# Second block of a two-block transformer: rounds cut into finer steps, queues reordered, projection tiles a round ahead, output halves in separate banks

## The reference, cut to what matters

```
a = rmsnorm(h, g_pre_mix);  u = a @ w_in
c_val, c_gate, q, k, v = split(u)                 # 512 columns each; 8 heads of 64
glu = c_val * sigmoid(c_gate)
y   = causal depthwise conv(glu, 31 taps) + conv_b          # 512 channels
conv_out = silu(layernorm(y))
z = q @ k.T / 8;  strictly causal mask
attn = exp(log_sigmoid(z) + reverse_cumsum_between(log_sigmoid(-z)))   # stick-breaking
attn_out = rmsnorm_per_head(attn @ v)
h = h + rmsnorm(concat(conv_out, attn_out) @ w_out)
h = h + rmsnorm((silu(f @ w_gate) * (f @ w_up)) @ w_down),  f = rmsnorm(h)
```

## Time and profile before

| what | us |
|---|---|
| three runs, median (lowest to highest) | 2006.15 (2003.53 to 2006.83) |
| the profiled execution | 2003.01 |
| its span in the trace | 2001.2 |
| PE busy in the span | 1849.5 (92%) |
| DVE busy | 957.3 (48%) |
| ACT busy | 769.7 (38%) |
| POOL busy | 159.7 (8%) |

### The profile page before, as it was taken

How to read it: one execution, slowest core, us unless ns; L and a number is a source line. 1 busy time by engine, 2 the same in 40 slices (tenths; PEclk the granted TensorE clock), 3 DMA queues, 4 the chain that set the end, 5 groups by cost and what they waited for, 6 DMA issues and landing times.

```text
span 2001.2 us, 21728 instructions
## 1 busy us (share of the span) xinstructions
PE 1849.5 (92%) x8477; PEld 1509.3 (75%) x8477; DVE 957.3 (48%) x1702; ACT 769.7 (38%) x1517; POOL 159.7 (8%) x204
## 2 busy tenths in 40 slices
...
GB/s 221 74 64 64 95 85 98 103 95 96 95 102 82 53 53 43 22 43 85 96 99 94 101 95 96 73 95 22 32 11 1 94 65 96 100 100 95 95 95 42
DMA packets 195749, 158.37 MB, mean 79 GB/s; under 512 B 5248, under 2 KB 161152, under 8 KB 195648
## 3 DMA queue, kind: packets, MB, share of 16 engines
...
## 4 chain that ended last, share of the span: by engine, by line
PE 80%; DVE 13%; ACT 5%; issue 2%; DMA 0%; SPq 0%; ACTq 0%; DVEq 0%
PE ps L727 26%; PE ps L728 25%; PE ps L729 25%; DVE sb L2174 3%; DVE sb L1779 2%; PE ps L777 1%; DVE sb L2293 1%; DVE sb L2225 1%; ACT sb L1626 0%; PE ps L1156 0%; DVE sb L1777 0%; DVE sb L1939 0%; PE ps L1044 0%; DVE sb L1805 0%; PE ps L1020 0%
## 5 line engine op out<-in xcount | busy, mean ns | idle before, releaser
L727 PE MATMUL ps<-sb,sb 128*128 128x512 f32 (+3 forms) x2547 | 1002.2, 396 | 45.3 <-DVE sb L2212 13.5
L728 PE MATMUL ps<-sb,sb 128*128 128x512 f32 (+3 forms) x2547 | 977.6, 386 | 0.0
L729 PE MATMUL ps<-sb,sb 128*128 128x512 f32 (+3 forms) x2547 | 977.1, 385 | 0.0
L727 PEld LDWEIGHTS ps<-sb,sb 128*128 128x128 f32 (+1 forms) x2547 | 486.2, 192 | 158.2 <-DVE sb L2212 14.4
L729 PEld LDWEIGHTS ps<-sb,sb 128*128 128x128 f32 (+1 forms) x2547 | 486.3, 192 | 94.2
L728 PEld LDWEIGHTS ps<-sb,sb 128*128 128x128 f32 (+1 forms) x2547 | 487.6, 193 | 87.8
L1779 DVE TENSOR_TENSOR sb<-sb,sb 128x512 fp32r<-128x512 f32 x532 | 356.2, 711 | 359.7 <-ACT sb L1292 358.6
L1292 ACT ACTIVATE sb<-sb 128x512 fp32r<-128x512 f32 x532 | 304.7, 622 | 453.6 <-PE ps L729 453.6
L1978 DVE TENSOR_TENSOR sb<-sb,sb 128x512 fp32r<-128x512 f32 x64 | 68.1, 1063 | 176.9 <-ACT sb L1434 176.9
L1444 ACT ACTIVATE sb<-ps 128x512 f32<-128x512 f32 x64 | 38.4, 599 | 208.3 <-PE ps L729 208.3
L633 POOL TENSOR_TENSOR sb<-sb 128x512 f32<-128x512 f32 x64 | 66.9, 1045 | 607.9 <-ACT sb L1444 607.9
...
## 6 DMA issues: line engine op xcount, KB each, us to landing
...
```

The costliest lines, as they stand in the source:

```text
L727: mm(ps, lh, rh, start=start, stop=False, **k)
L728: mm(ps, lh, rl, start=False, stop=False, **k)
L729: return mm(ps, ll, rh, start=False, stop=stop, **k)
```

## The change

The list `PLAN_C` is written anew, in these parts:

- **Tiles.** `v2` (the convolution's value tile), `q1` and `k1` move from the rounds into the fill phase, which now has twelve tiles. The four that are left (`q2 k2 q3 k3`) stand at the end of rounds 0 to 3, and the three convolution groups and `ln_sub` at the end of rounds 4 to 7 (`BEHIND`). Eviction (`ev`), splitting (`lo`) and weights (`w`) are steps of their own; a tile is evicted at the start of the next round.
- **Steps.** The ACT and DVE parts of `sp`, `bt` and `va` are cut: `sp` (DVE), `ex` (ACT exp of the head before), `sl` (split of the soft-plus), `ah` and `at` (split of the attention), `kp` (keep). PE runs `lg(u)`, `bt(u-1)`, `va(u-2)` and then the tile.
- **Diagonals.** ACT no longer builds any; POOL builds whole parts of a group at once with `tensor_tensor` on broadcast operands, high and low.
- **Pair sums** are made in bank 6 instead of bank 7, and `va` waits for their reading.
- **End.** The output product's slab order is pairs first (`[4,5],[6,7],[0,1],[2,3]`); its first slab is run early inside the list (`out_first`, step `o`); silu and its splits go row by row. Its second half accumulates in banks 4 to 7.

```diff
-    IN_FIRST = ["g0", "v0", "g3", "v3", "g1", "v1", "g2", "q0", "k0"]
-    IN_LATER = ["q1", "v2", "k1", "q2", "k2", "q3", "k3"]
+    IN_FIRST = ["g0", "v0", "g3", "v3", "g1", "v1", "g2", "v2", "q0", "k0", "q1", "k1"]
+    IN_LATER = ["q2", "k2", "q3", "k3"]
...
-        CH["out", n] = chunk([(W["w_out_2"][0], 512 * n, 512)], [[4, 5], [0, 1], [2, 3], [6, 7]])
+        CH["out", n] = chunk([(W["w_out_2"][0], 512 * n, 512)], [[4, 5], [6, 7], [0, 1], [2, 3]])
...
+        PLAN_C += [("tile", x), ("w", SL["in", x] + 3), ("ev", x), ("lo", x), ("taps", 5 if n >= 2 else 0)]
     for j in range(4):
+        PLAN_C += [("v2", j), ("w", CH["v2"].first + min(j, 2) + 3), ("taps", 4)]
     PLAN_C += [("v2_out",)]
+    BEHIND = [("tile", x) for x in IN_LATER] + [("cv", g) for g in range(3)] + [("ln_sub",)]
+    for u in range(8):
+        b = BEHIND[u - 1] if u else ("", "")
+        if b[0] == "tile":
+            PLAN_C += [("ev", b[1])]
+        elif b[0] == "cv":
+            PLAN_C += [("co", b[1])]
+        PLAN_C += [("lg", u), ("taps", 2)]
+        if u >= 4:
+            PLAN_C += [("pt" if u % 2 else "ps", u // 2 - 2)]
+        PLAN_C += [("taps", 2)]
+        if u >= 1:
+            PLAN_C += [("bt", u - 1)]
         if u >= 2:
             PLAN_C += [("va", u - 2)]
+        PLAN_C += [("sp", u)]
+        if u >= 1:
+            PLAN_C += [("ex", u - 1)]
+        if b[0] == "tile":
+            PLAN_C += [("lo", b[1])]
         if u >= 4 and u % 2 == 0:
+            PLAN_C += [("pr", u // 2 - 2)]
+        PLAN_C += [("sl", u)]
+        if u >= 1:
+            PLAN_C += [("ah", u - 1), ("at", u - 1)]
+        if u >= 2:
+            PLAN_C += [("kp", u - 2)]
+        PLAN_C += [BEHIND[u]]
+        if u < 5:
+            PLAN_C += [("w", CH["v2"].last + min(u, 3) + 4)]
+        if u >= 4 and u % 2:
+            PLAN_C += [("pl", u // 2 - 2)]
+        PLAN_C += [("taps", 2 if u < 6 else 100)]
+    PLAN_C += [("bt", 7), ("ps", 2), ("va", 6), ("ex", 7), ("pr", 2), ("o", (0, 1, 2)), ("ah", 7), ("at", 7), ("kp", 6),
+               ("ln_var",), ("pt", 2), ("ln_rs",), ("va", 7), ("kp", 7), ("pl", 2), ("ps", 3), ("pr", 3), ("ln_mul",),
+               ("o", (3,)), ("pt", 3), ("silu", 0), ("pl", 3)]
+    for j in range(1, 4):
+        PLAN_C += [("silu", j), ("ll", j - 1)]
+    PLAN_C += [("ll", 3)]
...
-                    e.tensor_scalar(DL[:, k % 16, :], IDENT, CWL[:, k:k + 1], None, ALU.mult).then_inc(S("dl"), 1)
+                    q.wait_ge(S("w_used"), SL["in", "k3"] + 1)
...
+                    if part[0] >= 16:
+                        q.wait_ge(S("cv_used"), 1 + (part[-1] >= 26))
...
+                    for dst, w in ((DH, CWH[:, at].bitcast(F32)), (DL, CWL[:, at])):
+                        TTT(dst[:, k0:k0 + n, :], eye, w.unsqueeze(2).broadcast_to([128, n, 128]), ALU.mult).then_inc(
...
-                act(ATh[:, :], TT[:, :], ACT.Copy).then_inc(S("at_hi"), 1)
-            elif kind == "va":
+            elif kind == "ah":
+                u = a[0]
                 q.wait_ge(S("sb_exp"), 3 * u + 3)
                 q.wait_ge(S("values"), u)
                 act(ATh[:, :], TT[:, :], ACT.Copy).then_inc(S("at_hi"), 1)
+            elif kind == "kp":
...
-        tile_n(CH["out", 0], M2h, M2l, mixed_ready, 0, lambda t: None)
-        tile_n(CH["out", 1], M2h, M2l, mixed_ready, 0, lambda t: q.wait_ge(S("f_ev"), t + 1))
+        tile_n(CH["out", 0], M2h, M2l, mixed_ready, 0, lambda t: None, done=1)
+        q.wait_ge(S("keep"), 8)
+        tile_n(CH["out", 1], M2h, M2l, mixed_ready, 4, lambda t: None)
```

More of the change, by code:

```diff
@@ L407, in build @@
     assert PAIR_NORMS == [("pair", s[1]) if s[0] == "pr" else ("ln",) for s in PLAN_C if s[0] in ("pr", "ln_rs")]
-    IN_7 = [s for i, s in enumerate(PLAN_C) if s[0] in ("cv", "ps", "pt", "ln_sub", "ln_var", "ln_mul")
-            or s[0] == "tile" and s[1] in IN_LATER]
+    IN_7 = [s for s in PLAN_C if s[0] in ("cv", "pt", "ln_sub", "ln_var", "ln_mul") or s[0] == "tile" and s[1] in IN_LATER]
     class Mem:
@@ L587, in out_of_7 @@
             return S("cv_ev"), step[1] + 1
-        if kind == "ps":
-            return S("rs_v"), USE["pair", step[1]] + 1
         if kind == "pt":
@@ L1231, in block_step @@
                 m.then_inc(S("ln_ps"), 1)
-        for step in PLAN_C:
-            block_step(*step)
         def mixed_ready(k):
```

149 lines of the change are left out of this document (69 added, 80 removed).

## The result

| | median, us | lowest to highest | runs |
|---|---|---|---|
| before | 2004.84 | 1997.91 to 2006.83 | 4 |
| changed | 1947.26 | 1946.32 to 1949.60 | 4 |

The ratio is 0.9721, with a 95% interval of 0.9695 to 0.9746: 2.8% faster. The forecast was 1943 us, with a range of 1931 to 1968. The profiled execution took 1949.6 us, its span is 1947.8 us, and PE is busy for 1833.5 us of it (94%).

What follows compares the result with a forecast made beforehand. The prediction took the order of work between fill phase and output product, where PE waits, as the bound. Its walk gave 62.9 us less: 2003.0 to 1940, plus 3.1 for the median, 1943 us; likeliest 1931 to 1952, with rivals to 1968.

Steps and rivals of the forecast that it cites:

- the likeliest case: Whole kernel: the forecast itself holds, 1931 to 1952 us, chance 0.62.
- the walk: Sum of stages from fill phase to output product's end, which moves from 1601.4 to 1538.5: 62.9 us less.
- Fill phase: Three more tiles before the first logits, paced by DVE: a cost of 19.3 us, first logits at 1356.6.
- the rival of a clock lost there: Fill phase: PE's short waits bring 1.2 GHz, some eight tiles slow down, 31 us more, 1974 us; chance 0.05.
- Round 0: First bank 7 tile still waits, until 1362.9, then takes 7.4 us; round 1 begins at 1370.3.
- Rounds 1 to 3: PE waits for nothing: 11.75 us for round 1, 13.75 each for rounds 2 and 3.
- 5 to 6 us to spare: Round 2 check: ACT's and DVE's splits `sl` and `at` are ready 5 to 6 us before PE needs them.
- Rounds 4 to 6: A convolution group and a `ps` or `pt` replace the tile: 16.5 us each, `pt` no longer stalls.
- 2.5 to 3.6 ns an element: Price taken for POOL's wide diagonal builds: first group 6.5 to 9.3 us against 9.4 available.
- hidden, or about 1 us late: POOL's diagonal builds before the convolution groups: they cost PE nothing or about 1 us.
- Tail: Logits of round 7 to output product's end: 79.4 us, last `pt` waiting for DVE until 36.6.
- Second half in its own banks: Output product's second half in separate banks: brings nothing, since PE had no gap between the halves.

Runs made afterwards that it cites:

- e11: Changed kernel with the weights and five taps around DVE's reading of the pair sums moved to the end of round 4; 1942.65 us, ratio 0.9690.
- e4: Kernel before with only the tiles moved: three into the fill phase, four to the end of rounds 0 to 3; 1982.26 us, ratio 0.9912.
- e7: Changed kernel with eviction and split of a late tile at the end of its own round instead of the next; 1953.93 us, ratio 0.9756.
- e3: Changed kernel with the old order of steps within a round (keep, soft-plus and its split first, then exp); 1960.12 us, ratio 0.9778.
- e10: Changed kernel with the pair's transposes (pt) of pairs 0 and 1 in the round of their sums, not one later; 1966.16 us, ratio 0.9811.
- e1: Changed kernel with POOL building 4 of 128 columns per diagonal and the convolution fed constant matrices (output wrong); 1942.87 us, ratio 0.9697.
- e2: Changed kernel with one tap more in each of rounds 0 to 3 and pair 1's split ahead of ln_sub; 1950.89 us, ratio 0.9718.
- e8: Changed kernel with all late taps in rounds 0 to 3 and pair 1's split ahead of ln_sub; 1945.98 us, ratio 0.9704.
- e5: Changed kernel without the early first slab of the output product; 1948.81 us, ratio 0.9731.
- e6: Changed kernel with both halves of the output product in banks 0 to 3; 1950.37 us, ratio 0.9748.
- e9: Changed kernel with the high diagonals built by ACT tap by tap and only the low ones by POOL; 1948.59 us, ratio 0.9725.

## Why the prediction was right, and which terms were off

The time fell in the likeliest case, and most terms of the walk came out. That the median was met to 4.3 us is in part luck: the walk put the stretch at 269.3 us (1269.2 to 1538.5) and it took 278.6, 9.3 more. The forecast had added 3.1 us to the walk because the profiled execution of before lay that much below its median; the profiled execution of the changed kernel lies 2.3 us above its own. The walk can be set beside the rows, stage by stage:

| stage | forecast | measured | e11 |
|---|---|---|---|
| fill phase, against before | +19.3 | +19.7 (68.4 to 88.1) | +19.6 |
| round 0 | 13.7 | 14.4 | 14.3 |
| rounds 1 to 3 | 39.25 | 38.8 | 38.9 |
| rounds 4 to 6 | 49.5 | 54.7 | 48.4 |
| tail | 79.4 | 82.5 | 82.2 |
| first logits to the end | 181.9 | 190.4 | 183.8 |

**Fill phase.** Right. PE's waits of 1.1 to 1.3 us, in four places, left the clock at 1.00; the rival of a clock lost there did not come, and e4 shows that the tiles' new places, these three and the four in rounds 0 to 3, bring 20.3 us by themselves.

**Round 0.** The wait for L2252 is 2.50 us where "about 3" stood; what stands ahead of the tile is 0.3 us shorter than forecast and the tile 1.0 longer, since the clock was at 0.50 for 5.8 us of it (1363.8 to 1369.6) and in the kernel before, where its 7.4 us came from, for 3.5 (1344.8 to 1348.3).

**Rounds 1 to 3.** PE waits for nothing, at 11.7, 13.6 and 13.6 us against 11.75, 13.75 and 13.75. The "5 to 6 us to spare" are real for the logits: in e7 the split comes at another place and these rounds do not move. What did not stand in my reckoning is that DVE's and ACT's order in these rounds decides where DVE is when round 4 begins (e3, e7).

**Rounds 4 to 6.** Rounds 5 and 6 are as forecast (15.6 and 16.8 against 16.5), and `pt` does not stall; e10 shows what that step is worth, 17.4 us. Round 4 is the term that was mis-sized: 22.3 instead of 16.5. I had POOL's builds priced at 2.5 to 3.6 ns an element and asked only whether PE would wait for them. They were cheaper than my lower end: the first four, 4096 elements, took 7.47 us with DVE nearly idle (e11, 1.82 ns an element) and 8.84 with DVE beside them (2.16), and PE never waited for them. The price fell on the other side, which I left out of the sum: I had read POOL's 1.86 against 1.30 us with DVE in its taps as a price for POOL alone. DVE lost 2.1 and 3.2 us in the rows above and 0.6 in the next two taps, then PE met the wait for the pair sums, which I had listed as a part of the change ("`va` waits for their reading") and never priced. The step that failed is "hidden, or about 1 us late": right for POOL's own consumer, wrong for the engine beside it. e1 and e11 give the size: a stretch of 271.9 and 272.0 against 278.6 and 275.7 of the changed kernel, 4 to 7 us, the slow clock included.

**Tail.** 82.5 against 79.4. It has a second wait for the reading of the sums (2.13 us), since the split of pair 1 stands ahead of it on DVE; with the split earlier (e2, e8) the wait is 0.82 and the tail 80.0, near the forecast. The early slab, for which I had made room in the walk, brings nothing (e5), because what ends last is the block of slabs behind the last `pt`. That `pt` waits for DVE as forecast, at 1505.2, 39.4 us into the tail where 36.6 stood; 168 matmuls follow in 41.1 us. Two small steps of the walk do not agree with their own prices, the values of head 6 (17.2 to 19.5, priced at 2.0) and the second slab (39.9 to 44.6, priced at 5.4); the slips nearly cancel.

**Second half in its own banks.** Nothing, as forecast (e6).

**What the gain is made of.** Taken back one at a time, the later `pt` costs 17.4 us of the stretch, the later split 9.9 (4.6 of them in rounds without a wait, by the clock), the step order 8.7; the tiles' places alone bring 20.3. These add up to more than 53.6; e3 and e7 pay in part for the same late reading in round 4 (waits of 6.96 and 5.83 us). How much of each is its own stays open. The bank of the pair sums, the slab order and the silu by rows were not taken back singly, and the diagonals' move to POOL only in part (e9). Also open: why the clock falls in some executions and not in others (last section), and the kernel that has e11's queue and the earlier split of pair 1 as well, which wasn't tried.
